# Dividing a tile's experts into two parts, so that rows of V are fetched by part

## The reference

```python
q = (xb @ w_query).reshape(TOKEN_BLOCK, PEER_HEADS, 2, PEER_DKEY // 2)
...
act = jax.nn.gelu(jnp.einsum('td,ted->te', xb, expert_u[eidx]), approximate=False)
return jnp.einsum('te,ted->td', gate.astype(xb.dtype) * act, expert_v[eidx])
```

## Time and profile before

| | |
|---|---|
| median of 3 runs | 3820.05 us |
| profiled execution | 3815.45 us, its span 3813.7 us |
| busy share: PE, DVE, ACT, POOL | 63%, 61%, 21%, 56% |
| bytes by the gathers' queue (q0), share of 16 DMA engines | 1140.99 MB, 77.1% |
| bytes by the queue of SP's loads (q1) | 130.17 MB, 9.1% |
| all bytes, mean rate over the span | 1273.81 MB, 334 GB/s |
| gathers issued by POOL | 2176 |

### The profile page before, as it was taken

How to read it: one execution, slowest core, us unless ns; L and a number is a source line. 1 busy time by engine, 2 the same in 40 slices (tenths; PEclk the granted TensorE clock), 3 DMA queues, 4 the chain that set the end, 5 groups by cost and what they waited for, 6 DMA issues and landing times. The chain is left out here.

```text
span 3813.7 us, 41357 instructions
## 1 busy us (share of the span) xinstructions
PE 2407.4 (63%) x13360; PEld 1520.5 (40%) x13360; DVE 2317.2 (61%) x6525; ACT 782.3 (21%) x2096; POOL 2138.7 (56%) x2180
## 2 busy tenths in 40 slices
PE   7876956776757854876668951865757850033355
PEld 6664746643424523654435621743524520000011
DVE  3464398877672369888672369887862369944400
ACT  3322225322021032322121032222121031000000
POOL 0000044666676665555664665666776666767775
PEclk9987978887878976988789975977978985556666
DMA  4100287999899998988998998999999999999999
GB/s 160 44 4 27 105 309 266 409 408 358 330 385 383 409 394 328 385 314 301 344 346 325 408 403 304 409 405 350 409 375 405 409 372 368 409 409 408 409 407 366
DMA packets 356427, 1273.81 MB, mean 334 GB/s; under 512 B 44698, under 2 KB 51930, under 8 KB 351476
## 3 DMA queue, kind: packets, MB, share of 16 engines
q0 software_dynamic: 313344, 1140.99, 77.1%
q1 hardware_dynamic: 42868, 130.17, 9.1%
HBM read 1265.91 MB, written 4.31 MB: 333 GB/s over the span
## 5 line engine op out<-in xcount | busy, mean ns | idle before, releaser
L3075 POOL DMA_INDIRECT slots<-in_peer_expert_u,table x1013 | 989.2, 976 | 1071.7 <-DVE table L2343 475.6
L3075 POOL DMA_INDIRECT slots<-in_peer_expert_v,table x1004 | 994.5, 990 | 461.9 <-issue 278.7
L1492 PE MATMUL ps<-slots,band 128*32 128x512 f32 x4016 | 729.4, 801 | 666.5 <-DMA slots<-in_peer_expert_v,table 585.2
L2464 DVE SCALAR_TENSOR_TENSOR slots<-slots,ps 128x1024 f32<-128x1024 f32 x564 | 668.2, 1216 | 157.6 <-DMA slots<-in_peer_expert_u,table 149.6
L1492 PEld LDWEIGHTS ps<-slots,band 128*32 128x32 f32 x4016 | 155.1, 131 | 1064.3 <-issue 1018.1
L2457 DVE SCALAR_TENSOR_TENSOR slots<-slots,xe 128x512 f32<-128x512 f32 x710 | 450.7, 687 | 99.9 <-DMA slots<-in_peer_expert_u,table 82.3
L874 PE MATMUL ps<-region_h,region_w 128*128 128x288 f32 (+1 forms) x1024 | 253.9, 406 | 13.8 <-DVE table L2428 13.8
L1432 PE MATMUL ps<-region_h,region_w 128*128 128x288 f32 (+1 forms) x1024 | 258.1, 406 | 0.0
L912 PE MATMUL ps<-arena,region_h 128*128 128x256 f32 (+5 forms) x1120 | 245.2, 376 | 14.6 <-ACT region_t L2626 10.8
L1432 PEld LDWEIGHTS ps<-region_h,region_w 128*128 128x128 f32 x1024 | 194.3, 195 | 82.8 <-issue 45.4
L874 PEld LDWEIGHTS ps<-region_h,region_w 128*128 128x128 f32 x1024 | 202.6, 199 | 58.7 <-issue 14.3
(11 more groups left out here) (497 smaller groups left out, 3813.5 us busy)
## 6 DMA issues: line engine op xcount, KB each, us to landing
region_w<-in_w_in SPq DMA_DIRECT2D x64, 512.0 KB, 7.0
region_w<-in_peer_w_query SPq DMA_DIRECT2D x64, 512.0 KB, 6.8
arena<-in_w_in SPq DMA_DIRECT2D x20, 1024.0 KB, 8.3
slots<-in_peer_expert_u,table POOLq DMA_INDIRECT x1013, 8.0
slots<-in_peer_expert_v,table POOLq DMA_INDIRECT x1004, 8.8
arena<-in_w_out SPq DMA_DIRECT2D x12, 1024.0 KB, 9.4
region_h<-in_w_out SPq DMA_DIRECT2D x4, 1024.0 KB, 8.7
region_v<-in_peer_sub_keys SPq DMA_DIRECT2D x8, 512.0 KB, 24.9
```

What stands on the lines that cost most here:

```text
L1492: mm = nc.tensor.matmul(ps[32 * j:32 * j + 32, 6 + half_, :], window(m % BAND, row), row_at((1, m), k.g)[:, half_ * 512:(half_ + 1) * 512] ...
L2464: V.scalar_tensor_tensor(rows, rows, 1.0, held, ALU.mult, ALU.mult, accum_out=own).then_inc(x_.u_free, 1)
L3075: G.indirect_dma_start(row_at(what, k.g), None, rows, bass.IndirectOffsetOnAxis(ap=numbers, axis=0)).then_inc(loaded[slot], 16)
```

## The change

A full tile's 128 experts are divided in two parts of EP = 64. A V gather then brings 64 experts of one token to partitions 0 to 63 and the same 64 experts of the token 16 further on to partitions 64 to 127, so a tile still has 128 V gathers, 64 for each part. Those of the first part are wanted as soon as the dots of U rows 0 to 63 are through the hand-over. The blocks of `eidT`, `wT` and `band` are laid out for this: each small copy moves 32 x 16 values instead of 32 x 32, and a band copy is made for each half of the partitions. The 8 matmuls of a batch stay; their stationary operand now has two filled columns, 16 apart, each over half the rows. A tile's sums go on over both parts, and there is still one closing add.

Since the sums now stand in PSUM banks 6 and 7 while the first tile's second part of U rows is being dotted, x for rows 64 to 127 of the first tile is read from `xe` in SBUF: in two halves in stages 1 and 2, whole in stage 0, and from PSUM banks 2 and 3 in stage 3. The diff, cut to its core:

```diff
+PARTS = 2
+EP, SPAN = P // PARTS, 32 // PARTS
 # Clock
+        self.cut = [(u, h) for u, c in enumerate(self.count) for h in range(PARTS if c == P else 1)]
+        self.part = [EP if c == P else DEC for u, _ in self.cut for c in [self.count[u]]]
+        self.begin = [self.first[u] + EP * h for u, h in self.cut]
-            wanted = u < len(self.spread) and now >= self.spread[u] + 2 * LAG - LAND
+            w = self.block(u, k)
+            wanted = w < len(self.spread) and now >= max(self.spread[w] + 2 * LAG - LAND, self.ahead + LAG)
-                if k == self.count[v] - 1:
+                if k % EP == EP - 1 or k == self.count[v] - 1:
                     self.gelu.append(now + LAND + LAG)
                     self.weigh.append(now + LAND + 2 * LAG)
                     self.spread.append(now + LAND + 3 * LAG)
+    def block(self, u, m):
+        return u * PARTS + m // EP
 # build
-        place = {"first": ps[:, 6:8, :]..., "second": ps[:, 0:2, :]...}
+        place = {"first": ps[:, 6:8, :]..., "rest": [ps[:, b:b + 2, :]... for b in (2, 0)]}
 # expert_sums
-                            row = b if batches == 32 else batches * j + b
+                            row = b if full else (batches * j + b) % SPAN
-                                                  start=(b == 0), stop=(b == batches - 1), skip_group_check=True)
+                                                  start=(h == b == 0), stop=(not full or h == PARTS - 1) and b == batches - 1,
+                                                  skip_group_check=True)
+        def divided(s, u, h):
+            return u < 2 and s < LAST and bool(u or s and h)
 # expert_dots
-                    elif u == 1 and k.s < LAST:
+                    elif divided(k.s, u, m // EP):
                         for b in range(2):
                             part = slice(512 * b, 512 * (b + 1))
                             ins = V.scalar_tensor_tensor(rows[:, part], rows[:, part], 1.0, xe[:, u, part], ALU.mult, ALU.mult,
-                                                         accum_out=(own, wT[1][:, m:m + 1])[b])
+                                                         accum_out=(own, wT[u][:, m:m + 1])[b])
-                        if m == P - 1:
-                            v.wait_ge(x_.u_free, k.last[u])
-                            V.tensor_tensor(dots[:, tok(1)], dots[:, tok(1)], wT[1], ALU.add).then_inc(x_.joined, 1)
+                        if m % EP == EP - 1:
+                            v.wait_ge(x_.u_free, k.first[u] + m + 1)
+                            w, more = dots[:, u * P + m + 1 - EP:u * P + m + 1], wT[u][:, m + 1 - EP:m + 1]
+                            V.tensor_tensor(w, w, more, ALU.add).then_inc(x_.joined, 1)
-                    v.wait_ge(x_.gelu_ready, tile + 1)
+                    v.wait_ge(x_.gelu_ready, block + 1)
+                    v.wait_ge(x_.idsT_ready, k.s + 1)
 # expert_weights
+                    a.wait_ge(route.top_done, 16)
+                    for t in range(2):
+                        A_.copy(place["rest"][t], xb[:, t, :]).then_inc(x_.placed, 1)
-                        for r in range(4):
-                            for c in range(4):
-                                ins = A_.copy(wT[u][DEC * c:DEC * (c + 1), DEC * r:DEC * (r + 1)], blocks[DEC * r:DEC * (r + 1), DEC * c:DEC * (c + 1)])
+                    for r in range(4):
+                        for c in range(EP // 32 if full else 1):
+                            for j in range(PARTS):
...
+                                src = blocks[32 * r:32 * (r + 1), src + SPAN * j:src + SPAN * (j + 1)]
+                                ins = A_.copy(wT[u % 2][row:row + 32, col:col + SPAN], src)
-                    ins = A_.copy(dst, src).then_inc(x_.band_ready, 1)
+                    for j in range(PARTS):
+                        R, at_ = slice(EP * j, EP * (j + 1)), first + SPAN * j
+                        ins = A_.copy(band[R, at_:at_ + 225:32].rearrange("p (i j) -> p i j", j=4), own[R])
+                    ins.then_inc(x_.band_ready, 1)
 # gathers
-                    token = u * P + m % 4 * (k.count[u] // 4) + m // 4
+                    w = k.block(u, m)
+                    token = u * P + EP * k.cut[w][1] + m % 4 * (k.part[w] // 4) + m % k.part[w] // 4
```

More of the change, by code:

```diff
@@ L214, in __init__ @@
             else:
-                now = self.spread[u] + 2 * LAG - LAND
+                now = max(self.spread[w] + 2 * LAG - LAND, self.ahead + LAG)
                 continue
             now += pace
+        assert self.n < 3 or self.spread[-1] > self.band[PARTS - 1][-1]
+    def block(self, u, m):
+        return u * PARTS + m // EP
     def beside(self, now):
@@ L445, in build @@
         ring += moved[0:1]
-        place = {"first": ps[:, 6:8, :].rearrange("p b n -> p (b n)"), "second": ps[:, 0:2, :].rearrange("p b n -> p (b n)")}
+        place = {"first": ps[:, 6:8, :].rearrange("p b n -> p (b n)"), "rest": [ps[:, b:b + 2, :].rearrange("p b n -> p (b n)") for b in (2, 0)]}
         LAST = len(STAGES) - 1
@@ L1471, in expert_sums @@
         def expert_sums(pe, k):
-            steps = sorted([(k.ahead, 0, 0, 0)] + [(due, 1, u, b) for u in range(k.n) for b, due in enumerate(k.batch[u])])
-            for due, kind, u, b in steps:
+            steps = sorted([(k.ahead, 0, 0, 0)] + [(due, 1, w, b) for w in range(len(k.cut)) for b, due in enumerate(k.batch[w])])
+            for due, kind, w, b in steps:
                 yield due
                 if kind == 0:
-                    for a in range(2):
-                        mm = nc.tensor.transpose(ps[:, 5, tok(a)], eid_f[:, tok(a)], ident)
+                    for a in range(2 * PARTS):
+                        mm = nc.tensor.transpose(ps[0:EP, 5, tok(a)], eid_f[:, EP * a:EP * (a + 1)], ident)
                     mm.then_inc(x_.ids_bank, 1)
                 else:
-                    first, batches = k.first[u] + 4 * b, k.count[u] // 4
+                    (u, h), batches = k.cut[w], k.part[w] // 4
+                    full, first = k.count[u] == P, k.begin[w] + 4 * b
                     if b == 0:
                         pe.wait_ge(x_.idsT_ready, k.s + 1)
-                        if k.tile0 + u:
+                        if h == 0 and k.tile0 + u:
                             pe.wait_ge(x_.acc_read, k.tile0 + u)
@@ L2435, in expert_dots @@
                     held = xe[:, u, :]
-                    if u == 0:
-                        summed[0] += 1
-                        if k.s == 0 or summed[0] > 2:
-                            held = place["first"]
-                            v.wait_ge(x_.placed, k.s + 1)
-                    elif k.s == LAST:
-                        held = place["second"]
-                        v.wait_ge(x_.placed, k.s + 2)
+                    summed[0] += 1
+                    if k.s == LAST and (u or m >= EP):
+                        held = place["rest"][u]
+                        v.wait_ge(x_.placed, k.s + 2 + u)
+                    elif u == 0 and m < EP and (k.s == 0 or summed[0] > 2):
+                        held = place["first"]
+                        v.wait_ge(x_.placed, k.s + 1)
                     v.wait_ge(loaded[places.slot(r)], places.landed(r))
@@ L2465, in expert_dots @@
                 elif kind == 2:
[L2466 to L2467 removed]
+                    block = k.block0 + k.block(u, EP * m)
+                    v.wait_ge(x_.gelu_ready, block + 1)
+                    v.wait_ge(x_.idsT_ready, k.s + 1)
                     if u < 2:
[L2469 removed]
+                        own = slice(u * P + EP * m, u * P + EP * (m + 1))
+                        w, g_ = dots[:, own], gate_e[:, own]
                     else:
@@ L2970, in expert_weights @@
                 yield due
-                tile = k.tile0 + u
-                full = k.count[u] == P
+                if 1 <= kind <= 3:
+                    block, (u, h) = u, k.cut[u]
+                    full = k.count[u] == P
                 if kind == 4:
@@ L3008, in expert_weights @@
                     first = column(8 * (chunk % 4))
-                    dst = band[:, first:first + 225:32].rearrange("p (i j) -> p i j", j=4)
-                    src = (wT[u] if full else blocks[:, 0:DEC]).rearrange("p (j i) -> p i j", j=4)[:, 2 * b:2 * b + 2, :]
-                    ins = A_.copy(dst, src).then_inc(x_.band_ready, 1)
-                    if not full and b == 3:
-                        a.wait_ge(x_.band_ready, chunk + 1)
-                        a.sem_inc(x_.wT_ready, 1)
+                    own = wT[u % 2][:, EP * h:EP * h + k.part[block]].rearrange("p (j i) -> p i j", j=4)[:, 2 * b:2 * b + 2, :]
+                    for j in range(PARTS):
+                        R, at_ = slice(EP * j, EP * (j + 1)), first + SPAN * j
+                        ins = A_.copy(band[R, at_:at_ + 225:32].rearrange("p (i j) -> p i j", j=4), own[R])
+                    ins.then_inc(x_.band_ready, 1)
         @block.scalar
```

62 lines of the change are left out of this document (35 added, 27 removed).

## The result

The changed kernel takes 3847.59 us, median of 4 runs (3838.66 to 3854.97), against 3819.49 for the kernel before; the ratio is 1.0073 with an interval of 1.0051 to 1.0095. (Intervals here are 95% intervals of the ratio to the kernel before, which was run again beside each set of runs.) Six further runs of it, beside the experiments, gave 3841.22 against 3820.12, ratio 1.0045 (1.003 to 1.0059). I had forecast 3812. The number lies at the upper end of my range, on the other side of the kernel before, and next to the 3848 of the rival "PE becomes the bound in A"; the experiments show that this agreement is one of numbers, not of mechanism.

A forecast was written before the change was run, and what follows sets the result against it. POOL's unbroken gather sequence was taken as the bound, with the DMA's ceiling at 409 GB/s. Terms -13 - 9 + 3 + 10 + 1 = -8 us gave 3807 for the profiled execution, 3812 against the median; range 3770 to 3848.

The forecast's parts named there:

- PE becomes the bound in A: Rival, chance 0.28: V batches entering each A overload PE, costing 28 us, or 3848.
- the new order: V gathers start 64 places earlier and U gathers end 64 later in each stage: -13 and -9 us.
- the pieces: Second-half dots from SBUF (+3 us) and a second hand-over per full tile (+10 on ACT, +1 on DVE).
- C: 64 late gathers per stage (digit: stage), V alone before, then half U: less waiting between PE and POOL, -9 us.
- The bound and the moved places: POOL's gather sequence sets the time, DMA floor unchanged; first V 64 places earlier, last U 64 later.
- A: 64 early gathers per stage (digit: stage), U alone before, then half V: DVE relieved, -13 us from stage 1.
- B: Stretch between A and C (digit: stage), U and V mixed before and after: no term of its own, 0.
- tail of stage 0: The stage's last gathers, V alone before and after; no term in the sum.
- The operand: x from SBUF for rows 64 to 127 of the first tile: +3 us on DVE, 0 on POOL's issue.
- Hand-overs: Two per full tile instead of one, with more table loads and small copies: +10 us ACT, +1 DVE.
- head of stage 0: The stage's first gathers, U alone, before A: taken as unchanged.
- My first rival: Chance 0.22: DVE's relief in A halves stage 1's 82 us loss in B, C gives 18: -45 us, 3775.

The follow-up runs named there:

- old_order: Changed kernel with the order of fetches of before, keeping both hand-overs, halves from SBUF and small copies; 3837.96 us, ratio 1.0037.
- all_halves: Changed kernel with every dot with x in SBUF made in two halves of 512 columns; 3831.48 us, ratio 1.0036.
- c_short: Changed kernel with the last 32 dots of stages 0 to 2 made over only part of the columns; 3826.90 us, ratio 1.0028.
- before_ops: Kernel before with x for rows 64 to 127 of the first tile from SBUF in stages 0 to 2; 3831.76 us, ratio 1.0037.
- late_v: Changed kernel with the first V row where it was before and three U rows, not four, between V batches; 3817.20 us, ratio 0.9988.
- six_u: Changed kernel with six U rows, not four, between batches of four V rows; 3855.40 us, ratio 1.0087.
- late_v_ps2: late_v with all x of the first tile in PSUM and stage 0's first hand-over due after the routing; 3799.98 us, ratio 0.9959.

## Why the prediction was wrong

The sum was -13 - 9 for the new order and +3 + 10 + 1 for the pieces it needs. The pieces cost about the 14 us that I had for them (old_order: 14, or 9 to 20, by the ratio, 18 by the medians), though not in the parts I had. The order was to give 22 us and gave nothing that can be told from zero: the change repeated stands 3 us above old_order. So the step that failed is the gain of the new order, with C's term above all, taken as -9 and measured as +28 in the repeat. By the first result, 28 us above the kernel before, the order would even cost some 14; the later six runs don't repeat that.

**The bound and the moved places** held. Stage 3 is unchanged (668 us, to within 3 in every kernel), the small copies and the first V gather are as worked out, and all losses and gains lie in stages 0 to 2.

**A, taken as -13.** In stage 1 the mechanism is there: PE's wait for L1658 (L1644 before), 22.1 us in the earlier trace rows, fell to 6.7, but A itself became 2 to 3 us longer and only B behind it 4 to 8 shorter, a net gain of 0 to 6 for my 13. Waits in 1567 to 1676 of the changed kernel:

```profile
POOL slots L3113 <- PE ps L1505: 20.1, 5, 9.7
...
PE ps L939 <- DVE region_v L1658: 6.7, 6, 2.7
```

POOL's 25.0 us behind DVE's dots became 20.1 us behind PE's batches: the wait changed its engine. In A of stage 0, where I wrote "nothing to win, 1 us at most", I left out that there was something to lose: 7 to 10 us, of which all_halves gives 2 to 5 back and the kernels with x of the whole first tile in PSUM all.

**C, taken as -9.** This is the step with the wrong sign: +26 us in the first profile, +28 in the repeat, with 7 to 9 given back in the tail of stage 0. I saw an idle DVE (24 of 110 us) and took it for one that frees U rows at once. It is idle because it waits, in order, for PE, and the wait stands ahead of the dots. And when it does dot them, it does so in instructions of the kind beside which an issue takes up to 1.99 us. c_short takes 18 of the 25 us of C0 and C2 away, all_halves 12 or 13; the 7 us that c_short leaves are put down to the order because nothing else is left, not by a run of their own.

**The operand, taken as 3 for DVE and 0 for POOL.** The row I read for the issue time, 1053 ns, was of halves, while in stage 0 and for the sample tile the change uses whole instructions. There the issue is up to 1.99 us, above the DMA's 1.28. My argument "1.24 against 1.28" would not have held for halves either: it took the undisturbed 0.94 us, and 1.05 with the 0.30 between two issues is 1.35. I had quoted the rule of the Trainium skill's page and set its price by a row of another form. Measured alone it is 14 us (8 to 21), ratio 1.0037. The extra 0.158 us of DVE a halved row was an overestimate: whole dots follow each other every 1.15 us, halves every 0.61 (both seen in before_ops above), so the extra is 0.08.

**Hand-overs, taken as 10 + 1.** About right: 15 us (9 to 21) with copies, the copies alone 5 (1 to 10), but with 7 of it in the head of stage 0, which I had declared untouched. Operand and hand-overs, 14 and 15 us each by itself, cost no more than 14 to 18 together; which wait they share is open.

**B, taken as 0.** It gave 13 us in the first profile and 22 in the repeat over the four stages. late_v and the kernels made from it, with fewer U rows in B of stage 1, show how much is in it: 22 to 25 us in that one stretch. My first rival named this place and a half of its 82 us of loss. Its mechanism, that DVE's relief in A lets B shrink, is not supported: the change relieves A and gains 4 to 8 us in B1, late_v leaves A as it was and gains 25.

**The rival whose number was met.** "PE becomes the bound in A" wanted eight batches at full price in each A. PE's busy share in A did rise: to 88.4 of 101 us in stage 2, where the DMA stayed at 409, and to 99.4 of 109 in stage 1, 91% and still below the 95 that the rival named. late_v, without V batches in A, has A1 and A2 of +3 and 0, the change +2 or +3 and -1 or +1. So its 46 us are not there, and that its 3848 was met is chance. Something near it does happen in six_u, whose POOL waits 42 us for PE in A of stage 1, but with a PE that is busy for 105 of 131 us: the batches stand late in PE's stream.

## What to carry to other kernels

An engine that looks idle may be waiting in order for the very engine it is to help; before moving work onto it, look at what stands ahead of that work in its stream, not at its busy share. When an operand moves from PSUM to SBUF, look for its price at the engine that issues gathers, and for the form of the instruction: 1024 columns in one instruction doubled the issue time, while two of 512 left most issues as they were and held a few for up to 4.9 us. And a reordering is best tried apart from the pieces it needs: here late_v_ps2, with the operand in PSUM again, the first V row where it was before, and three U rows instead of four between V batches, takes 0.41% off the kernel before, while the change as made adds 0.5 to 0.7%.

## What the runs showed of the hardware

A gather's issue on POOL takes 0.94 us when DVE reads x from PSUM, and up to 1.99 us beside back-to-back DVE instructions of 128 x 1024 with both operands in SBUF; with instructions of 128 x 512 from SBUF the issues after 668 us of all_halves are back at 0.94. The mean in 672 to 760 is 1190 ns for U gathers with whole instructions and 1046 with halves. But an issue can also last through a whole row of halves, 4.94 us in before_ops, and in A of stage 1 the mean beside halves is 1.15 us against 0.97. The times of a kernel also scatter more than I had taken them to: the kernel before took 3818 to 3821 us in the first three runs, and 3809.46 to 3826.34 in 32 runs beside one set of the experiments, so that single totals tell little under 10 us, while most stretches of the repeated change repeat within 2 us and all within 5.
